# Four projection blocks moved ahead of the index dots, and two row buffers for the rotations

## The chip, the cores and the metric

The kernel runs on one core of a Trainium2 chip. The metric is device time in microseconds of one execution. The times of before are those of three runs and their median; the profile is of one more execution.

## What is computed

Two transformer blocks follow one another on a sequence of 512 positions with 1024 features. The first has two layers. In each layer the normed input is projected to many heads at once, and four kinds of attention read them: A (with forget gates), B (each query attends to the 128 keys that an index selects), C (retention) and D (a sliding window). The part around the change computes the index of B and the forget sums of A:

```python
z = h @ w_in[l]                      # qA, kA, vA, fA, qB, kB, vB, qI, kI, wI, ...
logf = jax.nn.log_sigmoid((f_logit + f_bias).astype(jnp.float32))
F = jnp.cumsum(logf, axis=1)
...
dots = jnp.einsum('bqhd,bsd->bqhs', rope(qI), rope(kI))
score = jnp.einsum('bqhs,bqh->bqs', jax.nn.relu(dots), wI * w_scale)
_, sel = lax.top_k(score, topk)
...
# rope: x1, x2 are the halves of the 64 features of a head
rope(x) = concatenate([x1 * cos - x2 * sin, x2 * cos + x1 * sin])
```

The second block (a gated delta rule, a Fourier mixer and a convolved feed-forward) comes behind both layers; the change does not touch it.

## The kernel before

Features lie on the 128 partitions, the 512 positions on the free axis. Each projection is cut into tiles of 128 output features. Such a tile is eight blocks, one for each 128 input features, and a block is three matmuls of 128x128 weights with 512 columns (L977 to L979): high weights with high input, high weights with low input, low weights with high input. The weights come from DRAM twice: SyncE's queue loads `raw`, and POOL issues a DMA that rounds them into `weights_hi` (`issue`, L3370), for which there are three slots. POOL then subtracts the one from the other into `raw_lo` (`low`, L3384). A tile's first block waits until this subtraction is done.

The order of the blocks is a list made ahead (`Dense`, L151), and TensorE takes the next n of it wherever the program says `fill(n)` (L1036). Around the change the list runs tok, kIB (the keys kI and kB in one tile), qI 0, qI 1, q A 0, k A 0, v A 0, q A 1. The tiles go to PSUM banks in turn; q A 0 and v A 0 share bank 0, so v A 0 also waits for the copy of q A 0 out of it (`open_block`, L986).

Each engine runs its own written-out program, and they meet by semaphores alone. At the start of a layer (`pre`, one function for each engine):

- TensorE (L1156) fills up to the end of qI 1, turns the tile tok into `misc` (L1164), fills 12 blocks (q A 0 and half of k A 0), makes the forget sums F (L1172, L1173), waits for the rotated qI 1 (`rope_done`) and for the copies of the keys (`keys_copied`), and then makes six pairs of index dots (L1182), each followed by two blocks. Pairs 0 and 1 are 256 keys wide, 2 and 3 are 384, 4 and 5 are 512. All write the same PSUM tile `scores`; `free_scores` waits until the pair before has been read.
- A rotation takes four steps. ScalarE copies the halves of the tile crosswise into `swapped` (`swap`, L1837, four copies at L1844). VectorE multiplies the tile by the cosines (`rope_cos`, L2461). POOL multiplies `swapped` by the sines into `swapped_sin` (`swap_sin`, L3397). VectorE adds it (`rope_add`, L2467). There is one `swapped` and one `swapped_sin`: ScalarE's next swap waits for POOL's multiplication of the rotation before, and POOL's next multiplication for VectorE's addition of the one before. Rotations are numbered (`ROPE_NO`), kIB, qI 0, qI 1 first in a layer; there are 20 in a layer.
- ScalarE (L1902) copies `misc` to `tok` (L1904), swaps qI 0, makes Exp (L1908) and Ln (L1910) of the forget gates, swaps qI 1, copies the keys (L1897 to L1900) and F (L1914), and then makes the Relu of each pair (L1922), copying q A 0 (L1874) behind pair 0 and k A 0 (L1877) behind pair 3.
- VectorE (L2502) turns the first rotation, computes with the gates in small operations of 32 elements (L2511 reads `tok`, L2513 and L2518 follow), finishes the rotations of kIB, qI 0 and qI 1, and adds the Relus with their weights (L2532, L2535).
- POOL's order is in `norm_between` (L3467) and the loop at L3497: multiplication of kIB, `low` of k A 0, multiplication of qI 0, multiplication of qI 1, `issue` of v A 0 and q A 1, `low` of v A 0.

Of the kernel before, what the change touches and what calls it, by code (L numbers as in the profile page):

```python
# [18 lines left out]
ALU = mybir.AluOpType  # L19
# [6 lines left out]
TB = SEQ // P  # L26
HEAD_DIM, HEADS, IDX_HEADS, N_BRANCH = 64, 8, 4, 4
# [9 lines left out]
TOK_COLS = HEAD_DIM + HEADS + IDX_HEADS  # L37
# [230 lines left out]
ROPE_NO = {}  # L268
# [4 lines left out]


DOT_PAIRS = (TB - 1) * IDX_HEADS // 2
GROUP_SUMS_AFTER = 3
F_STEPS = 5
SCORE_GROUPS = {"A": ((0, 1), (2,), (3,)), "B": ((0, 1), (2,), (3,)), "D": ((0, 1), (2, 3))}
# [36 lines left out]
def misc_use(l, what):  # L315
    return l * len(MISC) + MISC.index(what)
# [66 lines left out]
KB_AT, KI_AT, VT_AT, V_AT, VD_AT, SW_AT, SWS_AT, PT_AT, P_AT = 77, 78, 79, 80, 82, 83, 84, 85, 92  # L383
# [21 lines left out]
def build_program(nc, x_in, stream, small_in, ada_in, cond_in, const_in, const2_in, wf_in, ctx_in, out):  # L405
    with ExitStack() as ctx:
# [13 lines left out]
        def region(name, at, n=1, dtype=F32):  # L420

            return nc.alloc_sbuf_tensor_at(name, [P, n, SEQ], dtype, offset=base + at * SEQ * 4)[:]

        def flat(t):
# [16 lines left out]
        v_flat = [v_all[:, n, :] for n in range(2)]  # L441
        kB, kI, kD, vt, vD_flat = (region(name, at)[:, 0, :] for name, at in (
            ("kB", KB_AT), ("kI", KI_AT), ("kD", KI_AT), ("v_feature", VT_AT), ("vD", VD_AT)))
        swapped, swapped_sin, f_rows = (region(name, at)[:, 0, :] for name, at in (
            ("swapped", SW_AT), ("swapped_sin", SWS_AT), ("f_rows", FROW_AT)))
        qI = region("qI", QI_AT, 2)
        gc = [region(f"gc{n}", at)[:, 0, :] for n, at in enumerate(GC_AT)]
        yc, ytok, ysq = (region(name, at)[:, 0, :] for name, at in (
# [523 lines left out]
        def _(pe):  # L972
# [63 lines left out]
            def fill(n):  # L1036

                for _ in range(n):
                    e = next(todo)
                    open_block(e)  # L1040
                    b = DENSE.bank[e.key]
                    at = slice(e.m * P, (e.m + 1) * P)
                    xl, xh = operand(e)
                    low = raw_lo(DENSE.items[e.item])[:, at]
                    high = ab_hi[:, e.m, :] if e.key[1] == "ab" else w_hi(DENSE.weights[e.item])[:, at]
                    to = banks[b]
                    if e.key[1] in ("ab", "qkv"):
                        to = to[:, 0:CTX if e.key[-1] else SEQ]
                    if e.key[1] == "ab":
                        to, low = to[0:AB, :], low[:, 0:AB]  # L1050
                    last = three_passes(to, low, high, xl, xh, e.k == 0, e.last)
                    if e.mark:
                        last.then_inc(dense_mark, 1)
# [102 lines left out]
            def pre(l):  # L1156
                if l:
                    pe.wait_ge(ada_read, 2 * l * ADA_L)
                fill(2 * KC if l else 2 * KC - 4)
                evac_wait((l, "tok"))  # L1160
                open_misc(l, "tok")
                pe.wait_ge(h_ready, 8 * (NORMS[(l, 1)] + 1))
                for t in range(TB):
                    last = nc.tensor.transpose(misc[:, t * TOK_COLS:(t + 1) * TOK_COLS],  # L1164
                                               vt[0:TOK_COLS, t * P:(t + 1) * P], ident[0:TOK_COLS, 0:TOK_COLS])
                last.then_inc(misc_ready, 1)
                fill(KC + 4)
                pe.wait_ge(f_dve, l * F_STEPS + F_STEPS)
                pe.wait_ge(rope_landed, 16)
                open_misc(l, "F")  # L1170
                to = misc[0:HEADS * TB, 0:P]
                nc.tensor.matmul(to, logf[:, 3, :], tri[:, 0:P], start=True, stop=False)  # L1172
                nc.tensor.matmul(to, logf[:, 0, :], ones, start=False, stop=True).then_inc(misc_ready, 1)  # L1173
                pe.wait_ge(rope_done, ROPE_NO[(l, "qI", 1)] + 1)
                pe.wait_ge(keys_copied, l * 5 + 5)
                for u in range(DOT_PAIRS):
                    i, pair = u // 2 + 1, u % 2
                    n = (i + 1) * P
                    free_scores(pe, l * S_LAYER + u)
                    for hh in range(2):  # L1180
                        half = slice(HEAD_DIM * hh, HEAD_DIM * (hh + 1))
                        last = nc.tensor.matmul(scores[:, hh, 0:n], qI[half, pair, i * P:(i + 1) * P], kI[half, 0:n],  # L1182
                                                start=True, stop=True)
                    last.then_inc(s_ready, 1)
                    fill(2)

            def attention(name, l, c):
                t = TURNS.index((name, c))
# [557 lines left out]
        def _(act):  # L1746
# [90 lines left out]
            def swap(key):  # L1837

                src, _ = result(key)
                r = ROPE_NO[key]  # L1840
                if r:
                    act.wait_ge(swap_mul, r)
                for q in range(4):
                    last = nc.scalar.activation(swapped[32 * q:32 * q + 32, :], src[32 * (q ^ 1):32 * (q ^ 1) + 32, :],  # L1844
                                                ACT.Copy)
                last.then_inc(swap_ready, 1)

# [481 lines left out]
        def _(dve):  # L2329
# [117 lines left out]
            def rope_dst(key):  # L2447
                l, prod = key[0], key[1:]
                if prod[0] == "qI":
                    return qI[:, prod[1], :]  # L2450
                if prod[0] == "kIB":
                    return kI
                if prod[:2] == ("k", "D"):
                    return kD
                return (qT if prod[0] == "q" else kT)[prod[2] % 2]
# [7 lines left out]
            def rope_add(key):  # L2463

                evac_wait(key)
                dve.wait_ge(swap_mul, ROPE_NO[key] + 1)
                nc.vector.tensor_tensor(rope_dst(key), rope_dst(key), swapped_sin, ALU.add).then_inc(rope_done, 1)  # L2467

            def branch_product(key):

# [31 lines left out]
            def pre(l):  # L2502
                if l == 0:
                    dve.wait_ge(rope_landed, 16)
                scale_tile((l, 1), 2)
                rope_cos((l, "kIB"))
                dve.wait_ge(misc_free, misc_use(l, "tok") + 1)
                z = logf[:, 0, :].rearrange("p (h t) -> p t h", t=TB)
                at = SMALL["forget_bias"] + l * HEADS
                bias = small[:, at:at + HEADS].unsqueeze(1).broadcast_to((P, TB, HEADS))  # L2510
                nc.vector.tensor_tensor(z, tok[:, :, HEAD_DIM:HEAD_DIM + HEADS], bias, ALU.add).then_inc(f_dve, 1)  # L2511
                dve.wait_ge(f_dve, l * F_STEPS + 1)
                nc.vector.scalar_tensor_tensor(out=logf[:, 1, :], in0=logf[:, 0, :], scalar=-1.0, in1=logf[:, 0, :],  # L2513
                                               op0=ALU.mult, op1=ALU.max).then_inc(f_dve, 1)
                rope_add((l, "kIB"))
                rope_cos((l, "qI", 0))
                dve.wait_ge(f_act, l * 5 + 2)
                nc.vector.scalar_tensor_tensor(out=logf[:, 3, :], in0=logf[:, 0, :], scalar=0.0, in1=logf[:, 2, :],  # L2518
                                               op0=ALU.min, op1=ALU.subtract).then_inc(f_dve, 1)
                sums_before(l)  # L2520
                rope_add((l, "qI", 0))
                rope_cos((l, "qI", 1))
                rope_add((l, "qI", 1))
                for u in range(DOT_PAIRS):
                    i, pair = u // 2 + 1, u % 2
                    n = (i + 1) * P
                    dve.wait_ge(s_free, l * S_LAYER + u + 1)
                    for hh in range(2):
                        at = HEAD_DIM + HEADS + 2 * pair + hh
                        w = tok[:, i, at:at + 1]  # L2530
                        if pair == hh == 0:
                            nc.vector.tensor_scalar(sel(i), prob(u, hh, n), w, None, ALU.mult).then_inc(score_step, 1)  # L2532
                        else:
                            dve.wait_ge(score_step, l * DOTS + 2 * u + hh)
                            nc.vector.scalar_tensor_tensor(out=sel(i), in0=prob(u, hh, n), scalar=w, in1=sel(i),  # L2535
                                                           op0=ALU.mult, op1=ALU.add).then_inc(score_step, 1)
                dve.wait_ge(score_step, (l + 1) * DOTS)
                for i in range(1, TB):
                    diag = sel(i)[:, i * P:(i + 1) * P]
                    nc.vector.tensor_tensor(diag, diag, causal, ALU.add).then_inc(topk_step, 1)  # L2540
# [821 lines left out]
        def _(pool):  # L3362
# [29 lines left out]
            def swap_sin(key):  # L3392
                r = ROPE_NO[key]
                pool.wait_ge(swap_ready, r + 1)
                if r:
                    pool.wait_ge(rope_done, r)
                nc.gpsimd.tensor_tensor(swapped_sin, swapped, sin, ALU.mult).then_inc(swap_mul, 1)  # L3397

            def add_square(name, step, n=SEQ):

# [484 lines left out]
```

## Time and profile before

| | us |
|---|---|
| median of three runs | 2864.16 (2862.68 to 2871.82) |
| the profiled execution | 2863.29 |
| its span, first to last instruction | 2861.5 |
| TensorE busy | 2816.0 (98%) |
| VectorE busy | 1509.8 (53%) |
| ScalarE busy | 771.6 (27%) |
| POOL busy | 1596.2 (56%) |

The granted clock of TensorE is 0.995 on average. A busy share says little about what a local change is worth; for that, the timelines of the engines in the stretch are read side by side. The two stretches here are 36 to 65 us (layer 0) and 1070 to 1097 us (layer 1). In a timeline the columns are start, duration, engine, line, operation, what is written and read, the count of merged instructions, and in brackets how long the engine was idle before and what released it.

### The profile page before, as it was taken

The numbers are of one execution on the slowest core, as the hardware profiler recorded it, in microseconds if no ns is written. First come the engines' busy times: TensorE is split into PE (matmuls) and PEld (weight loads), VectorE is DVE, ScalarE is ACT, GpSimd is POOL, SyncE is SP. The second block draws the span as 40 slices with busy tenths as digits, with TensorE's granted clock in tenths as the row PEclk, the third lists the DMA queues.
The fourth block names the chain that finished last, engine by engine and source line by source line (L and its number), as shares of the span: only waits on it lengthen the run. The fifth ranks groups of instructions, "written<-read, shape, count | busy, mean of one in ns | idle before, by whom it ended". The sixth has DMA issues, their size and how long they took to land.

```text
span 2861.5 us, 41070 instructions
## 1 busy us (share of the span) xinstructions
PE 2816.0 (98%) x16287; PEld 2268.6 (79%) x16287; DVE 1509.8 (53%) x2960; ACT 771.6 (27%) x1653; POOL 1596.2 (56%) x1116
## 2 busy tenths in 40 slices
PE   8999999999999999999999999999999999999998
PEld 5777778888888886777778888888878897788886
DVE  6663453247787126643542267884253566866601
ACT  5343332212211024343331122111032354311110
POOL 5444555667555564444556675556644554666664
PEclk9999999999999999999999999999999999999999
DMA  6444444545776554434445456775544101455554
GB/s 219 148 137 143 148 151 169 170 162 203 255 270 232 195 184 170 147 133 147 150 150 180 151 205 223 284 257 186 191 143 147 46 3 57 144 194 195 197 194 140
DMA packets 134064, 487.87 MB, mean 170 GB/s; under 512 B 15024, under 2 KB 16240, under 8 KB 133232
## 3 DMA queue, kind: packets, MB, share of 16 engines
q1 hardware_dynamic: 72096, 262.63, 27.6%
q0 software_dynamic: 60480, 220.23, 21.5%
q8 instruction: 130, 2.13, 0.3%
q10 hardware_dynamic: 1296, 2.37, 0.3%
q14 instruction: 62, 0.51, 0.1%
HBM read 483.04 MB, written 2.13 MB: 170 GB/s over the span
## 4 chain that ended last, share of the span: by engine, by line
PE 74%; issue 10%; POOL 9%; DVE 5%; ACT 1%; DMA 1%; SPq 0%; POOLq 0%; DVEq 0%; ACTq 0%
PE dense L977 20%; PE dense L979 20%; PE dense L978 20%; POOL raw_lo L3384 6%; PE scores L977 2%; PE scores L979 2%; PE scores L978 2%; POOL weights_hi L3370 1%; PE turned L1575 1%; PE turned L1587 1%; PE scores L1206 1%; PE O L1243 1%; POOL swapped_sin L3397 1%; PE turned L1231 1%; DVE neg_max L2604 0%
## 5 line engine op out<-in xcount | busy, mean ns | idle before, releaser
L3384 POOL TENSOR_TENSOR raw_lo<-raw,weights_hi 128x1024 fp32r<-128x1024 f32 x420 | 1011.3, 2408 | 39.5 <-DMA weights_hi<-stream 29.1
L977 PE MATMUL dense<-h_hi,weights_hi 128*128 128x512 f32 x2096 | 832.9, 397 | 5.5 <-DVE h_lo L2370 2.1
L3370 POOL DMA_DIRECT2D weights_hi<-stream x420 | 243.3, 579 | 1051.4 <-PE dense L979 950.4
L979 PE MATMUL dense<-h_hi,raw_lo 128*128 128x512 f32 x2096 | 817.9, 390 | 0.0
L978 PE MATMUL dense<-h_lo,weights_hi 128*128 128x512 f32 x2096 | 816.8, 390 | 0.0
L977 PEld LDWEIGHTS dense<-h_hi,weights_hi 128*128 128x128 f32 x2096 | 393.8, 188 | 104.5 <-issue 15.3
L979 PEld LDWEIGHTS dense<-h_hi,raw_lo 128*128 128x128 f32 x2096 | 393.7, 188 | 84.5
L978 PEld LDWEIGHTS dense<-h_lo,weights_hi 128*128 128x128 f32 x2096 | 394.4, 188 | 76.8
L977 PE MATMUL dense<-hidden_hi,weights_hi 128*128 128x512 f32 x528 | 205.7, 390 | 1.4 <-POOL raw_lo L3384 1.4
L978 PE MATMUL dense<-hidden_lo,weights_hi 128*128 128x512 f32 x528 | 205.4, 389 | 0.0
L979 PE MATMUL dense<-hidden_hi,raw_lo 128*128 128x512 f32 x528 | 205.4, 389 | 0.0
L3343 DVE SCALAR_TENSOR_TENSOR side_b<-scores,small_sb,side_b 128x441 f32<-128x441 f32 (+2 forms) x176 | 122.4, 695 | 65.9 <-ACT side_b L2308 60.5
L2562 DVE TENSOR_TENSOR y_parts<-O,y_parts 128x512 fp32r<-128x512 f32 x24 | 16.6, 691 | 230.5 <-ACT y_parts L1934 230.5
L2819 DVE SCALAR_TENSOR_TENSOR x<-dense,x 128x512 f32<-128x512 f32 x32 | 22.1, 692 | 219.9 <-PE dense L979 219.9
L977 PEld LDWEIGHTS dense<-hidden_hi,weights_hi 128*128 128x128 f32 x528 | 99.1, 188 | 22.2 <-POOL raw_lo L3384 1.8
L978 PEld LDWEIGHTS dense<-hidden_lo,weights_hi 128*128 128x128 f32 x528 | 99.1, 188 | 20.6
L979 PEld LDWEIGHTS dense<-hidden_hi,raw_lo 128*128 128x128 f32 x528 | 99.1, 188 | 20.6
L1844 ACT ACTIVATE swapped<-dense 32x512 f32<-32x512 f32 x144 | 84.9, 590 | 88.6 <-PE dense L979 87.3
L1959 ACT ACTIVATE probs<-probs,neg_max 128x128 f32<-128x128 f32 (+3 forms) x128 | 71.0, 556 | 118.2 <-DVE neg_max L2612 118.2
L977 PE MATMUL dense<-y_parts,weights_hi 128*128 128x512 f32 x256 | 102.3, 400 | 0.0
L1944 ACT ACTIVATE probs_turned<-turned 128x128 f32<-128x128 f32 (+2 forms) x192 | 68.3, 408 | 117.7 <-PE turned L1231 117.3
L978 PE MATMUL dense<-y_parts,weights_hi 128*128 128x512 f32 x256 | 99.9, 390 | 0.0
(528 smaller groups left out, 4534.0 us busy)
## 6 DMA issues: line engine op xcount, KB each, us to landing
raw<-stream SPq DMA_DIRECT2D x425, 512.0 KB, 3.3
weights_hi<-stream POOLq DMA_DIRECT2D x420, 512.0 KB, 4.5
ada_w<-ada SPq DMA_DIRECT2D x48, 512.0 KB, 5.2
gates<-f_scratch SPq DMA_DIRECT2D x2, 1536.0 KB, 9.0
x<-x_in SPq DMA_DIRECT2D x4, 512.0 KB, 7.2
cond_rows<-cond SPq DMA_DIRECT2D x2, 1024.0 KB, 6.7
decays<-stream ACTq DMA_DIRECT2D x8, 193.5 KB, 4.4
out<-x SPq DMA_DIRECT2D x3, 512.0 KB, 2.7
```

Source lines behind the costliest of these rows:

```text
L977: nc.tensor.matmul(to, wh, xh, start=first, stop=False)
L978: nc.tensor.matmul(to, wh, xl, start=False, stop=False)
L979: return nc.tensor.matmul(to, wl, xh, start=False, stop=final)
L1206: last = nc.tensor.matmul(scores[:, hh, to], qT[c % 2][half, i * P:(i + 1) * P], keys[half, k0:k1], start=(i == s), stop=True, skip_group_ ...
L1231: last = nc.tensor.transpose(turned[:, hh, m * P:(m + 1) * P], prob(i, hh, SEQ)[:, m * P:(m + 1) * P], ident)
L1243: last = nc.tensor.matmul(O[half, m * P:m * P + n], values[:, m, v0:v0 + HEAD_DIM], probT(hh, m, n), start=(m == 0), stop=True, skip_group ...
L1844: last = nc.scalar.activation(swapped[32 * q:32 * q + 32, :], src[32 * (q ^ 1):32 * (q ^ 1) + 32, :], ACT.Copy)
L1944: last = nc.scalar.activation(probT_step(hh, i, k0 // P, k1 // P), turned[:, hh, 0:k1 - k0].rearrange("p (m n) -> p m n", n=P), ACT.Copy)
L1959: last = nc.scalar.activation(prob(s, hh, n), src, ACT.Exp, bias=neg_max[:, at:at + 1], scale=QK_SCALE if name == "D" else 1.0, accum_out= ...
L3343: nc.vector.scalar_tensor_tensor(out=u, in0=v, scalar=small[:, tap:tap + 1], in1=u, op0=ALU.mult, op1=ALU.add).then_inc(conv_step if m < 7 ...
L3370: nc.gpsimd.dma_start(w_hi(w), stream[DENSE.items[DENSE.weight_list[w]]]).then_inc(hi_landed[s], 16)
L3384: nc.gpsimd.tensor_tensor(lo, src, hi, ALU.subtract).then_inc(weights_lo, 1)
```

## The change

TensorE takes four blocks ahead of the wait for the rotated qI 1, and 2, 1, 1, 1, 1, 2 behind the six pairs instead of two each. The rotations use two rows in turn; POOL multiplies in place. ScalarE's swap waits for the addition of the rotation two before, and POOL's wait for the addition before goes. VectorE's L2511 reads the gates in PSUM (`misc`) instead of their copy `tok`; its wait for that copy stays.

```diff
+FRONT_BLOCKS, DOT_BLOCKS = 4, (2, 1, 1, 1, 1, 2)
+assert FRONT_BLOCKS + sum(DOT_BLOCKS) == 2 * DOT_PAIRS
...
-        swapped, swapped_sin, f_rows = (region(name, at)[:, 0, :] for name, at in (
-            ("swapped", SW_AT), ("swapped_sin", SWS_AT), ("f_rows", FROW_AT)))
+        rope_rows = [region(f"rope_rows{n}", at)[:, 0, :] for n, at in enumerate((SW_AT, SWS_AT))]
+        f_rows = region("f_rows", FROW_AT)[:, 0, :]
...
                 nc.tensor.matmul(to, logf[:, 0, :], ones, start=False, stop=True).then_inc(misc_ready, 1)
+                fill(FRONT_BLOCKS)
                 pe.wait_ge(rope_done, ROPE_NO[(l, "qI", 1)] + 1)
...
                     last.then_inc(s_ready, 1)
-                    fill(2)
+                    fill(DOT_BLOCKS[u])
...
-                if r:
-                    act.wait_ge(swap_mul, r)
+                if r >= 2:
+                    act.wait_ge(rope_done, r - 1)
                 for q in range(4):
-                    last = nc.scalar.activation(swapped[32 * q:32 * q + 32, :], src[32 * (q ^ 1):32 * (q ^ 1) + 32, :],
+                    last = nc.scalar.activation(rope_rows[r % 2][32 * q:32 * q + 32, :], src[32 * (q ^ 1):32 * (q ^ 1) + 32, :],
                                                 ACT.Copy)
...
-                nc.vector.tensor_tensor(rope_dst(key), rope_dst(key), swapped_sin, ALU.add).then_inc(rope_done, 1)
+                nc.vector.tensor_tensor(rope_dst(key), rope_dst(key), rope_rows[ROPE_NO[key] % 2], ALU.add).then_inc(rope_done, 1)
...
+                gates = misc[:, 0:TB * TOK_COLS].rearrange("p (t n) -> p t n", t=TB)[:, :, HEAD_DIM:HEAD_DIM + HEADS]
...
-                nc.vector.tensor_tensor(z, tok[:, :, HEAD_DIM:HEAD_DIM + HEADS], bias, ALU.add).then_inc(f_dve, 1)
+                nc.vector.tensor_tensor(z, gates, bias, ALU.add).then_inc(f_dve, 1)
...
                 pool.wait_ge(swap_ready, r + 1)
-                if r:
-                    pool.wait_ge(rope_done, r)
-                nc.gpsimd.tensor_tensor(swapped_sin, swapped, sin, ALU.mult).then_inc(swap_mul, 1)
+                nc.gpsimd.tensor_tensor(rope_rows[r % 2], rope_rows[r % 2], sin, ALU.mult).then_inc(swap_mul, 1)
```

## Rows read from the trace of the kernel before

**Rows 1.** The page, busy time of each engine (us, share, instructions).

```profile
PE 2816.0 (98%) x16287; PEld 2268.6 (79%) x16287; DVE 1509.8 (53%) x2960; ACT 771.6 (27%) x1653; POOL 1596.2 (56%) x1116
```

**Rows 2.** Waits of TensorE: for whom, us in total, times, longest.

```profile
PE scores L1182 <- DVE qI L2467: 5.0, 2, 3.1
```

**Rows 3.** Timeline of TensorE in layer 0.

```profile
48.90 0.72 PE L1182 MATMUL scores<-kI,qI 64*128 64x256 f32 x4 [3.09 <-DVE qI L2467]
...
54.84 0.92 PE L1182 MATMUL scores<-kI,qI 64*128 64x384 f32 x4
55.69 0.50 PE L977 MATMUL dense<-h_hi,weights_hi 128*128 128x512 f32 x1
...
57.26 0.92 PE L1182 MATMUL scores<-kI,qI 64*128 64x384 f32 x4
...
62.34 1.13 PE L1182 MATMUL scores<-kI,qI 64*128 64x512 f32 x4
```

**Rows 4.** Stretches: length, engines' busy time (instructions), granted clock, DMA, GB/s.

```profile
1056.00:1066.00 10.00, 10.00 (x46) 8.29 (x45) 6.20 (x11) 5.58 (x11) 4.87 (x4) 1.00 0.50 166
49.50:52.90 3.40, 3.40 (x10) 2.31 (x10) 0.84 (x2) 1.15 (x3) 1.11 (x1) 0.50 0.90 305
```

**Rows 5.** Timeline of TensorE in layer 1.

```profile
1081.81 0.70 PE L1182 MATMUL scores<-kI,qI 64*128 64x256 f32 x4 [1.87 <-DVE qI L2467]
...
1084.03 0.70 PE L1182 MATMUL scores<-kI,qI 64*128 64x256 f32 x4
...
1086.25 0.92 PE L1182 MATMUL scores<-kI,qI 64*128 64x384 f32 x4
1087.50 0.47 PE L977 MATMUL dense<-h_hi,weights_hi 128*128 128x512 f32 x1 [0.34 <-POOL raw_lo L3384]
```

**Rows 6.** Timeline of POOL, layer 0 and the same subtraction in layer 1.

```profile
39.75 2.40 POOL L3384 TENSOR_TENSOR raw_lo<-raw,weights_hi 128x1024 fp32r<-128x1024 f32 x1
42.94 1.29 POOL L3397 TENSOR_TENSOR swapped_sin<-swapped,const 128x512 f32<-128x512 f32 x1 [0.80 <-DVE kI L2467]
46.79 1.26 POOL L3397 TENSOR_TENSOR swapped_sin<-swapped,const 128x512 f32<-128x512 f32 x1 [2.56 <-ACT swapped L1844]
...
51.78 2.36 POOL L3384 TENSOR_TENSOR raw_lo<-raw,weights_hi 128x1024 fp32r<-128x1024 f32 x1 [2.66 <-DMA weights_hi<-stream]
...
1084.99 2.37 POOL L3384 TENSOR_TENSOR raw_lo<-raw,weights_hi 128x1024 fp32r<-128x1024 f32 x1 [3.31 <-DMA weights_hi<-stream]
```

**Rows 7.** Timeline of ScalarE, layer 0 and qI 1's swap in layer 1.

```profile
42.58 1.28 ACT L1910 ACT_TABLE_LOAD   x1
...
44.32 2.39 ACT L1844 ACTIVATE swapped<-scores 32x512 f32<-32x512 f32 x4 [0.22 <-POOL swapped_sin L3397]
...
50.20 0.60 ACT L1874 ACTIVATE q<-dense 128x512 f32<-128x512 f32 x1
...
60.87 1.09 ACT L1922 ACTIVATE probs<-scores 128x512 f32<-128x512 f32 x2 [1.28 <-PE scores L1182]
...
1076.86 2.39 ACT L1844 ACTIVATE swapped<-scores 32x512 f32<-32x512 f32 x4 [0.33 <-POOL swapped_sin L3397]
```

**Rows 8.** Timeline of VectorE: small operations on the gates, layers 0 and 1.

```profile
39.90 2.30 DVE L2513 SCALAR_TENSOR_TENSOR logf<-logf 128x32 f32<-128x32 f32 x1
...
1071.17 3.33 DVE L2511 TENSOR_TENSOR logf<-sel_tok,small_sb 128x32 f32<-128x32 f32 x1 [1.21 <-ACT sel_tok L1904]
```

**Rows 9.** Timelines of VectorE and POOL in a turn of D, 345 to 351 us.

```profile
345.97 4.35 DVE L2604 SCALAR_TENSOR_TENSOR neg_max<-row_max,neg_sink 128x2 f32<-128x2 f32 x1
...
345.40 2.42 POOL L3384 TENSOR_TENSOR raw_lo<-raw,weights_hi 128x1024 fp32r<-128x1024 f32 x1
347.76 2.53 POOL L3451 TENSOR_TENSOR merged<-merged,gates 128x512 f32<-128x512 f32 x2
```

**Rows 10.** Tile `swapped`, whole span: idle before its instructions until whom (us, times).

```profile
  POOL swapped_sin L3397: 2.7, 4
  DVE kI L2467: 1.8, 2
```

## The prediction

> **What bounds the kernel now.** I read the page first. TensorE is busy for 2816.0 of 2861.5 us [rows 1], so the most that any reordering can give back is the 45.5 us in which it is not. The waits of TensorE then say where these are: the first index dot of each layer (L1182) waits for the rotation of qI, 5.0 us in two places, longest 3.1 [rows 2]. That is the place that this change works on. The third view is TensorE's timeline there. In layer 0 the dot starts at 48.90 after 3.09 us idle [rows 3], in layer 1 at 1081.81 after 1.87 [rows 5]. After the longer gap the granted clock is 0.50 from 49.5 to 52.9 us, 1.2 instead of 2.4 GHz [rows 4]; after 1.87 us of idleness it stays up. The price of the low stretch: from the first dot to the third takes 54.84 - 48.90 = 5.94 us in layer 0 [rows 3] and 1086.25 - 1081.81 = 4.44 in layer 1 for the same work [rows 5], so 1.50 us.
>
> A steady dense matmul costs 0.226 us: 46 touch a stretch of 10.00 us, each being 0.39 long, so 46 in 10.39 [rows 4]. A block of three is 0.68. All the change can remove is therefore 3.09 + 1.87 + 1.50 = 6.5 us, 0.23% of 2863.3.
>
> **Part 1, four blocks in front of the dots.** Twelve blocks stand behind the six pairs of dots, two each. They are the last four of k A 0 and the eight of v A 0. Four in front take 4 x 0.68 = 2.7 us: in layer 0 from some 45.8 (48.90 - 3.09) to 48.6, in layer 1 from 1079.9 to 1082.7. Both reach or pass the moment at which the dots were let go (48.90, 1081.81). So the wait for qI goes, and the first pair (0.7) ends at about 49.35 and 1083.45.
>
> What is late next decides the case. The first pair is now followed by v A 0, whose first block waits for its low weights, `low` of item 6 on POOL. That subtraction runs from 51.78 to 54.14, after 2.66 us of waiting for the weights_hi transfer, and from 1084.99 to 1087.36 in layer 1 [rows 6]. Before, four blocks of k and the pairs 1 and 2 stood between the first dot and this block: it started at 55.69 in layer 0, unhindered [rows 3], and at 1087.50 in layer 1, already 0.34 late on exactly this wait and 0.14 after the subtraction's end [rows 5]. The change doesn't touch POOL's order: the transfer of these weights is issued behind the multiplication of qI 1 (46.79), which waits 2.56 us for ScalarE's swap [rows 6]. So the stall isn't removed, it moves behind the first dot and grows: 54.28 - 49.35 = 4.9 us in layer 0 and 1087.5 - 1083.45 = 4.05 in layer 1, less what part 2 brings forward.
>
> What TensorE still has to do once v A 0 opens is more than before, since pairs 1 and 2 stand behind it. A pair costs what its period has beyond six dense matmuls (1.36): pair 1, 1086.25 - 1084.03 - 1.36 = 0.86 [rows 5]; pair 2, 57.26 - 54.84 - 1.36 = 1.06 [rows 3]. Together 1.92. The extra change between kinds of matmul lies in the stall and costs nothing; without it, some 0.2 a layer. The blocks behind v's opening are eight in both versions.
>
> One block between dots instead of two also uncovers ScalarE. The scores have one buffer, and a dot waits for the Relu of the pair before. The 512-wide Relu ends at 60.87 + 1.09 = 61.96 [rows 7]; with one block less the last pair would be due at 62.34 - 0.68 = 61.66 [rows 3]: 0.3 us of stall. The two places behind 384-wide pairs I put at 0.1 each, below that row. Sum 0.5, bounds 0.3 and 0.8.
>
> Layer 0: v opens at 54.28 instead of 55.69, -1.41; pairs +1.92; Relu +0.5; the low clock +1.50, since 4.9 us idle is more than the 3.09 that brought it. That is +2.5. Layer 1: opening 0, +1.92, +0.5, so +2.4; with 3.6 or more idle where 1.87 was, I count the low clock here too, +1.50 (between nothing and that; it lies nearer to the row with 3.09). Sum before part 2: +6.4 us.
>
> **Part 2, two row buffers.** POOL no longer waits for the key's addition before it multiplies qI 0 (0.80 us at 42.94 [rows 6]), and ScalarE no longer waits for POOL before it swaps. What counts is the swap of qI 1, at 44.32 and 1076.86 [rows 7], for everything up to v's low weights hangs on it: swap, multiplication, issue, transfer, subtraction. It now needs the addition to kI (`rope_done` of r - 1) and, in order on ScalarE, Exp, a table load of 1.28 us and Ln [rows 7]. Those begin when the small VectorE operation L2513 is done. Between 39.90 and 42.20 this took 2.30 us for 32 elements, while POOL's subtraction ran, and L2511 took 3.33 in layer 1, ending with POOL's at 1074.50 [rows 8]. **Part 3** lets L2511 read `misc`, which is PSUM, instead of `tok`. I take it as no longer held up; L2513 then comes 0.5 to 0.7 us before POOL's end of the multiplication and gets in there, as L2511 did in layer 0 (L2513 begins at 39.90 only because L2511 was done). Then the addition to kI is next, but POOL is in the subtraction until 42.15 [rows 6], and the multiplication of qI 0 is now ready behind it. In the row nearest to this a VectorE operation that started at 345.97 took 4.35 us, through the rest of POOL's subtraction and both operations that followed without a gap, to 350.3 [rows 9]. So I let POOL go first: 42.15 + 1.29 + 0.68 = 44.12 for the addition, and the swap starts at 44.15, 0.15 earlier. Layer 1: 1074.43 + 1.29 + 0.68 = 1076.4, 0.4 earlier. Bounds: -1.5 and +1.1 us in each layer (rivals 2 and 3). Both come off the opening of v: -0.55 together.
>
> The rotations of the attention and retention turns gain nothing: over the whole span and all its rotations ScalarE waited for POOL's row four times, 2.7 us, and POOL for VectorE's addition twice, 1.8 us [rows 10], and these are the places around the dots. The SP queue holds `f_rows` and the broadcast of F behind ScalarE; they move with the swap by the same tenths, and their reader, the first attention turn, comes behind all six pairs.
>
> **Sum.** 6.4 - 0.55 = +5.9 us: 2863.3 + 5.9 = 2869.2. The profiled execution stands 0.9 us under the median, 2864.2, so a median would be 2870; I say 2869.5.
>
> **Rivals.** (1) The weights are no obstacle, the change does what its words say. Then the next gate is bank 0: v A 0 writes where q A 0 lies, which ScalarE copies at 50.20 for 0.60, behind the first Relu [rows 7]. v would open at 50.75 and 1084.85: -4.94 + 1.92 + 0.5 = -2.5 in layer 0, without low clock, and -2.65 + 2.4 = -0.2 in layer 1. 2860.6. Against it stand the subtraction's rows, which would have to end 3 us sooner; for it, nothing but an order that I misread. 0.08.
>
> (2) The addition to kI gets in when POOL's subtraction ends, as it waited first. The swap then starts at 42.15 + 0.68 = 42.85 and 1074.43 + 0.68 = 1075.1 at best, 1.5 and 1.7 earlier, less where Ln is later; I take 1.4 each. 5.0 (both layers, low clock in the first alone, as 2.6 idle in the second lies between 1.87 and 3.09) - 2.8 = +2.1: 2865.4. The Trainium skill (SBUF — State Buffer, Who interferes with whom) has this rule: VectorE with two SBUF inputs and a GpSimd operation that reads SBUF exclude each other, and who issues first goes first; with at most one SBUF input there is no clash, which is what part 3 relies on. The long VectorE rows agree with the exclusion; the row that ran through three POOL operations speaks against "first come". 0.22.
>
> (3) The other side, slower beyond the measurement: L2513 misses the gap at POOL's multiplication, as L2511 did in layer 1 (it began at 1071.17 and ended only at 1074.50), and misses the next too, because POOL no longer pauses there. It is done at 43.6 and 1075.9; with Exp, load and Ln, 1.8 us, the swap starts at 45.4 and 1077.7, 1.1 and 0.85 later. 6.4 + 1.95 + 0.5 (upper ends of the Relu stalls) = +8.9: 2872.2. It decides from two missed gaps in both layers. 0.12.
>
> **Chances.** Forecast 0.50, rival 1 0.08, rival 2 0.22, rival 3 0.12, and 0.08 for what I haven't seen. About 0.3% (8.6 us) is what a measurement of this kernel can tell from no change. Only rival 3 and some of the unseen lie beyond it: slower 0.12, faster 0.02, same 0.86. The range takes in rivals 2 and 3 with a median's spread: 2862.5 to 2874.
>
> **What would show it.** The first dot of each layer starts without a wait; the first dense matmul behind it waits some 4 us for POOL's raw_lo; the clock is at 0.50 behind it in both layers; qI 1's swap starts at 44.1 and 1076.4 relative to the same work; L2511 takes some 0.2 us; small waits for ScalarE's Relu stand before the last three pairs. The prediction is wrong if v A 0 opens before 52 us in layer 0, or if TensorE has a new wait outside of these two places.

## The result and the profile after

| | before | after |
|---|---|---|
| median of 16 runs each, us | 2864.24 (2861.74 to 2871.82) | 2871.04 (2868.03 to 2875.95) |
| ratio to before | | 1.0024, 95% interval 1.0018 to 1.0031 |
| the profiled execution, us | 2863.29 | 2870.90 |
| its span, us | 2861.5 | 2868.7 |
| TensorE busy, us | 2816.0 | 2820.9 |

The changed kernel takes 6.8 us longer, 0.24%. The interval excludes no change; its upper end, 0.31%, stands at the 0.3% within which the prediction called the time the same.

The waits of TensorE after (for whom, us in total, times, longest) no longer hold the index dot's wait for qI of [rows 2]. The first line is another one:

```profile
PE dense L979 <- POOL raw_lo L3388: 10.5, 7, 4.0
PE turned L1578 <- POOL a_level L3571: 2.4, 2, 1.3
```

TensorE's timeline after, layer 0 and layer 1, in answer to [rows 3] and [rows 5]:

```profile
34.99 0.29 PE L1166 MATMUL misc<-const,v_feature 76*128 76x76 f32 x1 [0.30 <-ACT v_feature L1883]
...
47.75 0.70 PE L1185 MATMUL scores<-kI,qI 64*128 64x256 f32 x4
52.04 0.47 PE L979 MATMUL dense<-h_hi,weights_hi 128*128 128x512 f32 x1 [3.59 <-POOL raw_lo L3388]
...
53.89 1.22 PE L1185 MATMUL scores<-kI,qI 64*128 64x256 f32 x4
...
58.50 0.92 PE L1185 MATMUL scores<-kI,qI 64*128 64x384 f32 x4
...
62.02 0.40 PE L981 MATMUL dense<-h_hi,raw_lo 128*128 128x512 f32 x1
62.70 1.13 PE L1185 MATMUL scores<-kI,qI 64*128 64x512 f32 x4 [0.29 <-ACT probs L1925]
...
1070.77 0.43 PE L1166 MATMUL misc<-const,v_feature 76*128 76x76 f32 x4
...
1083.41 0.70 PE L1185 MATMUL scores<-kI,qI 64*128 64x256 f32 x4
1088.14 0.77 PE L979 MATMUL dense<-h_hi,weights_hi 128*128 128x512 f32 x1 [4.03 <-POOL raw_lo L3388]
```

The first dot of each layer starts without a wait, and the block of v A 0 behind the first pair waits 3.59 and 4.03 us for its low weights. Stretches after (length, busy time of the engines, granted clock, DMA):

```profile
53.20:56.60 3.40, 3.40 (x10) 1.38 (x8) 0.72 (x2) 0.66 (x2) 1.62 (x1) 0.50 1.02 355
1087.40:1097.70 10.30, 9.56 (x24) 5.00 (x24) 2.00 (x4) 1.53 (x4) 3.50 (x3) 0.50 0.92 353
```

Half clock (0.50, 1.2 GHz) for 3.4 us in layer 0, as in [rows 4], and for 10.3 us in layer 1, where before there was none. The timeline shows TensorE at work in most of both: 3.40 and 9.56 us.

POOL's timeline, layer 0 and layer 1, in answer to [rows 6]:

```profile
38.74 2.41 POOL L3388 TENSOR_TENSOR raw_lo<-raw,weights_hi 128x1024 fp32r<-128x1024 f32 x1
41.10 1.75 POOL L3399 TENSOR_TENSOR rope_rows<-rope_rows,const 128x512 f32<-128x512 f32 x1
...
49.56 2.34 POOL L3388 TENSOR_TENSOR raw_lo<-raw,weights_hi 128x1024 fp32r<-128x1024 f32 x1 [2.69 <-DMA weights_hi<-stream]
...
1074.91 1.27 POOL L3399 TENSOR_TENSOR rope_rows<-rope_rows,const 128x512 f32<-128x512 f32 x1
1080.54 1.30 POOL L3399 TENSOR_TENSOR rope_rows<-rope_rows,const 128x512 f32<-128x512 f32 x1 [4.35 <-ACT rope_rows L1847]
...
1085.66 2.34 POOL L3388 TENSOR_TENSOR raw_lo<-raw,weights_hi 128x1024 fp32r<-128x1024 f32 x1 [2.74 <-DMA weights_hi<-stream]
```

VectorE's, in answer to [rows 8]:

```profile
38.07 0.20 DVE L2515 TENSOR_TENSOR logf<-misc,small_sb 128x32 f32<-128x32 f32 x1
38.30 0.54 DVE L2517 SCALAR_TENSOR_TENSOR logf<-logf 128x32 f32<-128x32 f32 x1
38.90 2.80 DVE L2470 TENSOR_TENSOR kI<-kI,rope_rows 128x512 f32<-128x512 f32 x1
...
1071.94 4.30 DVE L2517 SCALAR_TENSOR_TENSOR logf<-logf 128x32 f32<-128x32 f32 x1
1076.16 0.68 DVE L2470 TENSOR_TENSOR kI<-kI,rope_rows 128x512 f32<-128x512 f32 x1
```

ScalarE's swap of qI 1 in both layers, in answer to [rows 7]:

```profile
42.05 2.40 ACT L1847 ACTIVATE rope_rows<-scores 32x512 f32<-32x512 f32 x4
...
1078.07 2.40 ACT L1847 ACTIVATE rope_rows<-scores 32x512 f32<-32x512 f32 x4
```

L2515 (was L2511) takes 0.20 us where it took up to 3.33 [rows 8]. In layer 0 L2517 (was L2513) is done in 0.54 us, and the addition to kI gets in as POOL's subtraction ends at 41.15: it is done at 41.70, and POOL's multiplication, begun at 41.10, takes 1.75 instead of 1.29 us. In layer 1 L2517, the same instruction at the same place, takes 4.30 us: its record spans the rest of the multiplication of kIB, the whole subtraction and the multiplication of qI 0.

**One ruler for all kernels.** The executions differ by up to 1 us before the stretch is reached (tok is turned at 35.99 before, at 34.99 after). So I measure, in each profile, from the start of the turning of tok to the first score of turn A 0. Before this is 64.98 - 35.99 = 28.99 us in layer 0 and 1096.89 - 1070.24 = 26.65 in layer 1; after it is 30.36 and 33.33. Together +8.05 us; less the 1.0 of the earlier start that is +7.05 of the span's +7.2. The other 0.15 lie outside the two stretches.

### The profile page after: what moved, and what is told of

Read it like the earlier page. It is cut to its first block, busy times and chain, and to the rows that moved or that the text cites. A ratio compares the mean times of both kernels' runs of the same rounds, so it can differ in the third digit from the quotient of the medians.

```text
span 2868.7 us, 41031 instructions
## 1 busy us (share of the span) xinstructions
PE 2820.9 (98%) x16287; PEld 2269.9 (79%) x16287; DVE 1505.8 (52%) x2960; ACT 771.6 (27%) x1653; POOL 1597.2 (56%) x1116
## 4 chain that ended last, share of the span: by engine, by line
PE 71%; issue 12%; POOL 10%; DVE 4%; ACT 1%; DMA 1%; POOLq 0%; SPq 0%; DVEq 0%; ACTq 0%
PE dense L979 19%; PE dense L981 19%; PE dense L980 19%; POOL raw_lo L3388 7%; PE scores L979 2%; PE scores L980 2%; PE scores L981 2%; POOL weights_hi L3374 2%; PE turned L1578 1%; PE turned L1590 1%; PE O L1246 1%; DMA weights_hi<-stream 1%; PE scores L1209 1%; POOL rope_rows L3399 1%; DVE neg_max L2608 0%
## 5 line engine op out<-in xcount | busy, mean ns | idle before, releaser
L1847 ACT ACTIVATE rope_rows<-dense 32x512 f32<-32x512 f32 x144 | 84.9, 590 | 88.6 <-PE dense L981 87.2
L979 PE MATMUL dense<-y_parts,weights_hi 128*128 128x512 f32 x256 | 102.3, 400 | 0.0
L981 PE MATMUL dense<-y_parts,raw_lo 128*128 128x512 f32 x256 | 99.9, 390 | 0.0
```

The costliest lines, as they stand in the source:

```text
L979: nc.tensor.matmul(to, wh, xh, start=first, stop=False)
L981: return nc.tensor.matmul(to, wl, xh, start=False, stop=final)
L1847: last = nc.scalar.activation(rope_rows[r % 2][32 * q:32 * q + 32, :], src[32 * (q ^ 1):32 * (q ^ 1) + 32, :], ACT.Copy)
```

## The experiments

W is the theory of the prediction: v A 0's low weights are the new gate, pairs 1 and 2 come to stand behind it, and the clock falls in the wait. Its rival R was that the two rows cost the time, because operations of POOL and VectorE hold each other up; theories C and G and the other rivals are told in the expectations that name them. The stretches are by the ruler above; the ratio is to before, with its 95% interval. A stretch is that of one profiled execution.

| kernel | layer 0 | layer 1 | sum less before | median | ratio |
|---|---|---|---|---|---|
| before | 28.99 | 26.65 | | | |
| after | 30.36 | 33.33 | +8.1 | 2871.04 | 1.0024 (1.0018 to 1.0031) |
| order alone | 32.10 | 29.86 | +6.3 | 2872.59 | 1.0029 (1.0019 to 1.0040) |
| rows alone | 27.75 | 27.78 | -0.1 | 2863.80 | 1.0002 (0.9993 to 1.0010) |
| early weights | 28.18 | 31.50 | +4.0 | 2868.39 | 1.0017 (1.0008 to 1.0026) |
| pairs first | 26.96 | 29.52 | +0.8 | 2865.48 | 1.0006 (0.9997 to 1.0015) |
| kept busy | 28.80 | 29.31 | +2.5 | 2866.48 | 1.0014 (1.0005 to 1.0023) |
| POOL waits | 30.38 | 32.79 | +7.5 | 2872.36 | 1.0028 (1.0017 to 1.0040) |
| early copy | 26.05 | 25.41 | -4.2 | 2859.51 | 0.9987 (0.9978 to 0.9996) |
| two in front | 25.04 | 24.62 | -6.0 | 2857.65 | 0.9980 (0.9972 to 0.9989) |
| one row | 26.28 | 24.94 | -4.4 | 2859.80 | 0.9986 (0.9977 to 0.9994) |
| gates from the copy | 26.00 | 24.61 | -5.0 | 2860.05 | 0.9985 (0.9976 to 0.9993) |
| POOL goes on | 25.02 | 27.80 | -2.8 | 2860.18 | 0.9988 (0.9979 to 0.9997) |

The median of before was 2864.24 beside after, 2863.92 beside the next four kernels, 2863.12 beside the four from kept busy on, and 2863.79 beside the last three. Where medians of two groups are compared below, I also give the difference of their distances to before.

The length of the low clock differs between executions of one kernel. Of the 84 executions of before beside the eleven experiments, the 19 with a mean granted clock of 0.993 or 0.994 took 2866.0 us in the median, the 65 with 0.995 or 0.996 2863.4. So where a stretch holds a low clock, its size is that of the one execution that was profiled.

### The order alone, the rows alone

The first takes the order of the blocks and leaves the rotations and gates as they were. The second is the reverse, and this is its edit against after:

```diff
-FRONT_BLOCKS, DOT_BLOCKS = 4, (2, 1, 1, 1, 1, 2)
+FRONT_BLOCKS, DOT_BLOCKS = 0, (2, 2, 2, 2, 2, 2)
```

> The order of the blocks alone (four in front, then 2, 1, 1, 1, 1, 2), with one row of each kind and the gates read from tok, as before. Theory W (v A 0's low weights are the new gate, pairs 1 and 2 stand behind it, and the clock falls): the weights are ready when they were before, so TensorE idles some 4.9 us in layer 0 and 4.0 in layer 1 behind the first pair of dots, the clock is at 0.50 behind both, and the whole takes 6 to 9 us longer than before, at least as long as the changed kernel. Rival R (the two row buffers cost the time, because POOL and VectorE collide at L2517 and L2470, and the order is harmless): 0 to 5 us shorter than before.

> The two row buffers and the gates read from PSUM alone, with the order of blocks of before (no block in front, two behind each pair). Theory W: TensorE still waits for qI 1 at the first dot; the swap of qI 1 starts 1.3 us earlier where VectorE gets between POOL's operations and up to 0.7 later where it doesn't, so between 3 us shorter and 1 us longer than before. Rival R: most of the 7 us of the changed kernel stay, 4 to 7 us longer than before.

The order alone costs all of it: 2872.6 beside 2863.9. TensorE's timeline:

```profile
53.66 0.76 PE L978 MATMUL dense<-h_hi,weights_hi 128*128 128x512 f32 x1 [4.61 <-POOL raw_lo L3386]
...
1089.45 0.76 PE L978 MATMUL dense<-h_hi,weights_hi 128*128 128x512 f32 x1 [3.43 <-POOL raw_lo L3386]
```

v A 0 waits 4.61 us in layer 0 (4.9 expected) and 3.43 in layer 1 (4.0 expected), and the clock is at half speed for 6.8 and 3.4 us there. The rows alone give nothing in sum: 1.2 us shorter in layer 0, 1.1 longer in layer 1, where the first dot comes 12.26 instead of 11.57 us after tok's turning and v A 0 waits 0.78 us instead of 0.34. R falls: the rows alone don't cost the time. What they add to the order isn't settled: the stretches of after are 1.7 us longer than those of the order alone, its distance to before is 1.9 us shorter (6.8 beside 8.7), and the two executions had the low clock for different times (3.4 and 10.2 us, and 6.8 and 3.4). The expectation for the rows was a range with both signs; what it didn't say is that the gain and the loss are tied to the layer.

### Early weights

```diff
+                if what == ("q", "A", 0):
+                    issue(w + 2)
                 if what != ("qI", 1):
                     finished(w - 2)
-                if what in (("k", "A", 0), ("up", 2, 1)):
+                if what == ("up", 2, 1):
                     issue(w + 1)
```

> The changed kernel with POOL issuing the transfer of v A 0's weights ahead of qI 0's multiplication instead of behind qI 1's; no work is left out. Theory W: the transfer lies under ScalarE's swap of qI 1, the subtraction ends some 3.5 us earlier in layer 0 and 1.5 to 3 in layer 1. v A 0 then opens behind the copy of q A 0, some 1.3 us after the first pair in layer 0, and with an idle time of 1 to 2 us in layer 1; the clock stays up. 8 to 10 us shorter than the changed kernel, 1 to 4 us shorter than before. Rival R: the collisions stay, so within 1 us of the changed kernel.

Only 2.6 us of the 8 to 10 came (2.3 by the distances to before, 4.0 in the stretches). The timeline of TensorE in layer 0 shows two waits in place of the one:

```profile
49.41 0.70 PE L1185 MATMUL scores<-kI,qI 64*128 64x256 f32 x4 [1.53 <-DVE qI L2470]
51.36 0.50 PE L979 MATMUL dense<-h_hi,weights_hi 128*128 128x512 f32 x1 [1.25 <-ACT q L1877]
```

POOL's timeline, and below it VectorE's, show where the first comes from:

```profile
46.41 2.39 POOL L3388 TENSOR_TENSOR raw_lo<-raw,weights_hi 128x1024 fp32r<-128x1024 f32 x1
```

```profile
45.97 3.38 DVE L2470 TENSOR_TENSOR qI<-qI,rope_rows 128x512 f32<-128x512 f32 x1 [0.68 <-POOL rope_rows L3399]
```

The weights were ready, v A 0 never waited for them. But the subtraction, now earlier, runs across the addition of qI 1, which takes 3.38 us instead of 0.69, and the first dot waits for it. The second wait is the copy of q A 0 out of bank 0, which rival 1 of the prediction had named. In layer 1 the two waits are 2.57 and 1.24 us, and the clock, expected to stay up, is at 0.50 for 6.8 us. W's gate is confirmed, but the expectation of what its removal gives was too high: behind it stood two more.

### Pairs first

```diff
-FRONT_BLOCKS, DOT_BLOCKS = 4, (2, 1, 1, 1, 1, 2)
+FRONT_BLOCKS, DOT_BLOCKS = 4, (0, 0, 2, 2, 2, 2)
```

> The changed kernel with pairs 0, 1 and 2 back to back behind the four blocks and then 2, 2, 2, 2 (blocks behind pairs 2 to 5). Theory W: pairs 1 and 2 (1.9 us a layer) now lie in the wait for v A 0's weights instead of behind it, v A 0 opens at the same time as in the changed kernel, the Relu stalls of the last pairs go (0.3 a layer), and the low clock costs as much or less: 4 to 7 us shorter than the changed kernel, 0 to 3 us longer than before. If instead the term for the pairs is wrong, nothing is gained, as dots back to back wait for the Relu (0.7 us each).

It tests the term of 1.92 us for the pairs behind the wait. TensorE's timeline:

```profile
49.28 0.70 PE L1185 MATMUL scores<-kI,qI 64*128 64x256 f32 x4 [0.76 <-ACT probs L1925]
50.74 0.92 PE L1185 MATMUL scores<-kI,qI 64*128 64x384 f32 x4 [0.76 <-ACT probs L1925]
52.10 0.47 PE L979 MATMUL dense<-h_hi,weights_hi 128*128 128x512 f32 x1 [0.45 <-POOL raw_lo L3388]
```

v A 0 opens where it did (52.10 beside 52.04), each pair waits 0.76 for the Relu, and all of that lies inside the wait that is there anyway; in layer 1 v A 0 waits 1.26. Layer 0 is 3.4 us shorter than after. The clock stays up there; the next run prices that at 1.56 us, which leaves 1.8 for the pairs (1.92 in the prediction). In layer 1 the clock still falls, for 6.8 us. The median is 5.6 shorter (5.2 by the distances to before), within the 4 to 7 expected.

### Kept busy

```diff
                     last.then_inc(s_ready, 1)
+                    if u == 0:
+                        pe.wait_ge(s_init, INITS)
+                        pe.wait_ge(evacuated[DENSE.bank[(l, "v", "A", 0)]], evac_count((l, "v", "A", 0)) - 1)
+                        idle_products(banks[DENSE.bank[(l, "v", "A", 0)]], 14)
```

> The changed kernel with 14 idle matmuls (bf16, 384 columns, into bank 0, which v A 0 overwrites) between the first pair and v A 0, behind the wait for the copy of q A 0; nothing is left out. It prices the clock alone: v A 0 opens when it did. If the low clock behind the stall costs what I take it to (1.5 us in layer 0; in layer 1, where it was low for 10.2 us, some 4), the granted clock stays at 1.00 in both stretches and the whole is 4 to 6 us shorter than the changed kernel, 1 to 3 us longer than before. If the clock falls all the same or is worth nothing, it is within 1 us of the changed kernel.

TensorE's timeline in layer 0:

```profile
49.86 2.44 PE L986 MATMUL dense<-masks 128*128 128x384 bf16 x14 [1.34 <-ACT q L1881]
52.08 0.47 PE L979 MATMUL dense<-h_hi,weights_hi 128*128 128x512 f32 x1
```

and the granted clock of both stretches, 1.00:

```profile
48.50:64.00 15.50, 13.71 (x62) 6.96 (x61) 7.86 (x11) 6.22 (x15) 5.26 (x3) 1.00 0.79 283
1082.00:1099.00 17.00, 14.84 (x70) 7.39 (x68) 6.24 (x12) 6.71 (x15) 5.50 (x4) 1.00 0.77 273
```

v A 0 opens at 52.08 beside 52.04, so this is the clock alone: 30.36 - 28.80 = 1.56 us in layer 0 and 33.33 - 29.31 = 4.02 in layer 1, where v A 0 opened 0.13 later by the ruler (17.50 beside 17.37), so that the clock's price is nearer 4.1. The median is 4.6 shorter than after, within the 4 to 6 expected; by the distances to before it is 3.4 (3.4 above before, where 1 to 3 was expected). Useless matmuls in a wait make a kernel faster here.

### POOL waits

```diff
                 pool.wait_ge(swap_ready, r + 1)
+                if r:
+                    pool.wait_ge(rope_done, r)
```

> The changed kernel with POOL's wait for the addition of the rotation before restored (two rows still, ScalarE's wait as changed). Theory C (in layer 1 the small operation L2517 misses two gaps between POOL's operations because POOL no longer pauses): L2517 or the addition to kI gets in behind POOL's subtraction, 1.3 us sooner in layer 1, the swap of qI 1 and v A 0's weights come 1.3 us sooner there, and layer 0 stays as it is: 1 to 3 us shorter than the changed kernel (more than the 1.3 only if the clock falls for less time). If removing the wait was harmless, the same as the changed kernel or up to 0.5 us longer.

The mechanism is as theory C has it, its time isn't. VectorE's and ScalarE's timelines in layer 1:

```profile
1071.79 3.08 DVE L2517 SCALAR_TENSOR_TENSOR logf<-logf 128x32 f32<-128x32 f32 x1
```

```profile
1076.69 2.40 ACT L1847 ACTIVATE rope_rows<-scores 32x512 f32<-32x512 f32 x4
```

L2517 in layer 1 takes 3.08 us instead of 4.30, and the swap of qI 1 starts 5.33 us after the first block of q A 0 instead of 6.57. But v A 0 opens only 0.44 us sooner (16.20 beside 16.64 from that first block), since the transfer of its weights took 4.6 us from issue to landing in this execution and 3.7 in that of after. The stretch is 0.5 us shorter, where 1 to 3 was expected. The median is no shorter (2872.4 beside 2871.0, intervals overlapping). The profiled execution is even 2.4 us longer than that of after, and that comes from the second block, which neither kernel changes: there the granted clock is 0.50 from 2476.5 to 2490.0 us, where in the execution of after it is 1.00 up to 2480. What the pause is worth was thus left for the last run.

### Early copy, and two in front

Both take the early transfer, POOL's wait as restored above, and put POOL's subtraction behind qI 1's addition. The first also copies q A 0 ahead of the first Relu; the second leaves the copy in its place and changes the order. The fence has what both do on POOL and then the second's order:

```diff
                     issue(w + 1)
+                    if what == ("v", "A", 0):
+                        pool.wait_ge(rope_done, ROPE_NO[(l, "qI", 1)] + 1)
                     low(w)
...
-FRONT_BLOCKS, DOT_BLOCKS = 4, (2, 1, 1, 1, 1, 2)
+FRONT_BLOCKS, DOT_BLOCKS = 2, (2, 1, 1, 2, 2, 2)
```

> The kernel with the early transfer of v A 0's weights, and besides: POOL's wait restored, POOL's subtraction of v A 0 behind the addition of qI 1 instead of across it, and q A 0 copied ahead of the first Relu. Theory W with the collision that the run before showed: the first pair starts without a wait, v A 0 opens within 1 us of its end in both layers, the clock stays up. 9 to 12 us shorter than the changed kernel, 2 to 5 us shorter than before. If something else than these three gates holds v A 0, a wait of over 1.5 us stands in front of it.

> As the kernel with the early copy, but q A 0's copy in its old place, two blocks in front of the first pair and 2, 1, 1, 2, 2, 2 behind the six. v A 0 then stands behind the second pair, some 2 us later in TensorE's order, and behind both the weights and the copy. Theory W: no wait of over 0.5 us in either stretch, the clock stays up, 4 to 6.5 us shorter than before. If the order of the blocks in front itself costs more than it hides, it is no shorter than before.

With the three gates seen to (the transfer, the subtraction across qI 1's addition, the copy of q A 0), four blocks in front are 3.6 us shorter than before (v A 0 waits 0.75 and 0.23 us). With two in front v A 0 stands behind pair 1, and nothing waits for it. TensorE's timeline in layer 0:

```profile
46.72 0.70 PE L1185 MATMUL scores<-kI,qI 64*128 64x256 f32 x4 [0.22 <-DVE qI L2470]
...
48.94 0.70 PE L1185 MATMUL scores<-kI,qI 64*128 64x256 f32 x4
49.58 0.50 PE L979 MATMUL dense<-h_hi,weights_hi 128*128 128x512 f32 x1
50.47 0.92 PE L1185 MATMUL scores<-kI,qI 64*128 64x384 f32 x4
```

and POOL's there:

```profile
46.76 2.38 POOL L3388 TENSOR_TENSOR raw_lo<-raw,weights_hi 128x1024 fp32r<-128x1024 f32 x1 [0.36 <-DVE qI L2470]
```

The subtraction is done at 49.14, v A 0 opens at 49.58. This version beats both kernels: 2857.65, ratio to before 0.9980 (0.9972 to 0.9989), 5.5 us shorter than before in the same runs.

### What the parts are worth there

Three kernels take one thing away from the version with two in front: the second row and the gates (one row of each kind, gates from tok), the gates alone, POOL's pause alone. The edit of the gates alone:

```diff
-                nc.vector.tensor_tensor(z, gates, bias, ALU.add).then_inc(f_dve, 1)
+                nc.vector.tensor_tensor(z, tok[:, :, HEAD_DIM:HEAD_DIM + HEADS], bias, ALU.add).then_inc(f_dve, 1)
```

> The kernel with two blocks in front and the early transfer, but with one row of each kind and the gates read from tok, as in the kernel before. It asks what the second row and the gates are worth where nothing else stands in the way. By the spans from tok's turning to the first dot (12.91 and 11.57 us before, when qI 1 was what it waited for) the first dot waits some 1.4 us longer in layer 0 and 0.3 in layer 1 than with two rows (11.68 and 11.27): 1 to 3 us longer than the kernel with two rows, 2.5 to 5 us shorter than before. If the rows and the gates are worth nothing, within 0.5 us of the kernel with two rows.

> The kernel with two blocks in front, early transfer and two rows, with L2515 reading the gates from tok again. Theory G (the read from PSUM is what lets the small operation behind it into POOL's first gap in layer 0): L2517 takes some 2.3 us in layer 0 again, Exp and the swap of qI 1 come later, the first dot of layer 0 waits 1.0 to 1.5 us; layer 1, where the gap is missed anyway, changes by under 0.3. 1 to 1.5 us longer than the kernel with two rows. Rival: no change, because the swap of qI 1 waits for something else.

> The kernel with two blocks in front, early transfer and two rows, without POOL's wait for the addition of the rotation before (as in the changed kernel). Theory C: in layer 1 L2517 misses the second gap too (4.3 us instead of 3.1), the swap of qI 1 comes 1.2 us later, and the first dot, which had no wait there, waits some 1 us; layer 0 is the same. 0.5 to 1.5 us longer than the kernel with the wait. Rival (the pause buys nothing): the same within 0.3 us in the stretch of layer 1.

By the stretches, all three came as expected in kind. One row: +1.24 in layer 0, +0.32 in layer 1; the first dot waits 1.48 and 0.27 us. Gates from the copy: +0.96 and 0; L2515 takes 0.80, L2517 2.30, the dot waits 1.20 in layer 0. So of the 1.24 that rows and gates give in layer 0, the gates bring 0.96 and the second row the other 0.3. POOL without its pause: 0 in layer 0, +3.2 in layer 1, where 0.5 to 1.5 was expected: L2517 takes 4.96 us, the dot waits 1.58, and behind that wait the clock is low for 3.4 us. VectorE's and POOL's timelines in layer 1, first with the pause (two in front), then without it (POOL goes on):

```profile
1066.51 3.09 DVE L2517 SCALAR_TENSOR_TENSOR logf<-logf 128x32 f32<-128x32 f32 x1
1069.50 0.60 POOL L3374 DMA_DIRECT2D weights_hi<-stream  x1
1070.37 1.29 POOL L3401 TENSOR_TENSOR rope_rows<-rope_rows,const 128x512 f32<-128x512 f32 x1 [0.27 <-DVE kI L2470]
...
1066.61 4.96 DVE L2517 SCALAR_TENSOR_TENSOR logf<-logf 128x32 f32<-128x32 f32 x1
1069.58 0.60 POOL L3374 DMA_DIRECT2D weights_hi<-stream  x1
1070.21 1.30 POOL L3399 TENSOR_TENSOR rope_rows<-rope_rows,const 128x512 f32<-128x512 f32 x1
```

In both POOL issues the transfer for 0.60 us between its subtraction and its next multiplication. With the pause L2517 is done there, at 1069.60; without it, it isn't done before 1071.57, as the multiplication ends. So it is the wait in the program that lets VectorE in, not the 0.6 us between two operations; why, no run here shows.

The medians are 2.2 to 2.5 us above that of two in front (1.5 to 1.9 by the distances to before). The ratios' intervals overlap with its, so the sizes rest on the stretches of single executions, and of the 3.2 the part that is the clock's is that of this execution.

## Why the prediction was right, and where not

The time was forecast at +5.9 and came at +6.8, inside the range, and within 0.3%, the case with 0.86. Point by point:

- **The gate.** Right. v A 0's first block waits for POOL's subtraction in both layers, 3.59 and 4.03 us (some 4.8 and 3.6 forecast with part 2). Only moving the transfer took this wait away; with the pairs first it was filled, down to 0.45 and 1.26 us.
- **Pairs 1 and 2 behind it, 1.92 us.** Right: taken back in front, they bring 1.8 us in layer 0, inside the wait.
- **The Relu, 0.5 a layer.** Right. The idle times at the waits, 0.29 us twice, are short of it, as they count from a modelled end. By the starts, a pair that waits for nothing begins 0.32 us after the last matmul before it. In layer 0 the last three pairs begin 0.48, 0.48 and 0.68 us after it, 0.7 more in sum; in layer 1 the last two begin 0.47 and 0.67 after it, 0.5 more.
- **The clock, 1.5 in each layer.** Right in layer 0 (1.56). In layer 1 the term was mis-sized: 4.0 to 4.1. I took the price of the one low stretch of rows 4, 3.4 us long; this one lasted 10.3. The thought that an idle time between 1.87 and 3.09 us decides it, which rival 2 used, didn't hold either: in the rows alone the clock fell behind 1.79 us of idleness in layer 0 and stayed up behind 2.52 in layer 1.
- **Part 2, the step that failed.** I let POOL's multiplication go ahead of the addition to kI in both layers. In layer 0 the addition got in (rival 2), the swap of qI 1 came 42.05 - 34.99 = 7.06 us after tok's turning instead of 8.33: 1.27 earlier, not 0.15. In layer 1 L2517 missed both gaps (rival 3), and the swap came at 7.30 instead of 6.62: 0.68 later, not 0.4 earlier. Both lie within the bounds of -1.5 and +1.1 that I gave, and the two errors, 1.1 us each, took each other back.
- **By layers**, +1.4 us in layer 0 (2.35 forecast) and +6.7 in layer 1 (3.5 forecast). In layer 1 2.6 of the difference is the clock; the rest is mostly v A 0, which opened 0.1 us later than before (17.37 beside 17.26 by the ruler) and not 0.4 earlier. The two stretches together took 8.1 us more, the sum said 5.9. That the spans differ by only 7.2, and the medians by 6.8, is luck: errors of opposite sign, and a start that was 1.0 us earlier in the one profile.
- **The signs.** v A 0 opened at 52.04 in layer 0, 17.05 us after tok's turning, which is 53.04 in the time of before; the sign of being wrong was "before 52". Beside the waits for v A 0 the list of waits has only those for the Relu as new ones, 0.6 us in two places. The swaps of qI 1 didn't come when forecast, see part 2.
- **"L2511 is no longer held up."** Right, 0.20 and 0.22 us; and the run that undid it alone lost 1.0 us in layer 0.

The Trainium skill (SBUF — State Buffer, Who interferes with whom) says that a VectorE instruction with at most one SBUF input, outside the 2-port modes, does not contend with GpSimd, which is POOL. These rows agree: L2515 took 0.20 and 0.22 us, and 0.80 and 3.33 with both inputs in SBUF. The page also says that issue order decides who blocks. That held in layer 0 for kI's addition. It did not hold in layer 1, where L2517 began its wait at 1071.94 and POOL's subtraction (from 1072.55) and multiplication (from 1074.91) both went ahead of it.

## What to carry to other kernels

Before moving work in front of a wait, ask what the next work behind the wait needs, and when: here it was a transfer queued behind the very chain that one was waiting for. Moving the front blocks without their weights turned 5 us of waiting into 7.6. Put the transfer ahead first, then choose how many blocks to move so that each gate is passed before TensorE reaches it. Here two did better than four, by 1.8 us in the two stretches and 1.9 in the medians (whose intervals overlap), though the two kernels also differ in where q A 0 is copied. A wait on a helper engine that looks idle may be what lets another engine in; taking it out is a change to the order of both.

## What the runs showed of the hardware that was not expected

- The same 32-element operation of VectorE (L2517), which comes while POOL is in its multiplication with its subtraction next, took 0.53 or 0.54 us in layer 0 in all nine kernels that read the gates from PSUM. In layer 1 it took 3.08 or 3.09 with POOL's pause (three kernels) and 4.30 to 4.96 without (six). With and without the pause the outcome was the same in every profile; what decides it, no run here shows.
- After waits of 3.6 and 4.0 us in the same kernel the granted clock was at 0.50 for 3.4 and 10.3 us, while TensorE was busy for 3.40 and 9.56 us of them. The long one cost 4 us, as much as the wait before it. Why it lasted longer stays open; filling the wait with idle matmuls avoided it.
- The length of the wait doesn't tell what the clock does. In POOL waits, waits of 3.58 us (layer 0) and 3.62 (layer 1) were followed by 3.4 and 10.2 us at 0.50. Waits of 1.58 us (POOL goes on, layer 1) and 1.79 (rows alone, layer 0) were followed by 3.4 us of it, waits of 1.87 (before, layer 1) and 2.52 (rows alone, layer 1) by none.
- The 512 KB transfer of v A 0's weights in layer 1 took 3.7 us from issue to landing in the execution of after and 4.6 in that of POOL waits, which issued it at the same place in its program.
